# Hybrid trunk on one core: the folded attention matrices are built head by head inside the four mixer tiles

## The reference

```python
SEQ, D_MODEL, N_MEM, HEADS, D_FF = 2048, 1024, 256, 4, 2816
mem_n = rms_norm(mem, mem_norm)
h = rms_norm(x, mix_pre_norm)
zp, za, zg, zb, zc, zx = split(h @ w_in)          # 256, 384, 384, 384, 384, 384 columns
ya = pool_mixer(zp, pool_maps, pool_scale)        # causal means over 2, 4, 8, 16 rows
yb = silu(layer_norm(dwconv31(za * sigmoid(zg)) + b))
yc = zb * dwconv3(zc * zx)
x  = x + rms_norm(concat(ya, yb, yc) @ w_out, mix_post_norm)
h  = rms_norm(x, xattn_pre_norm)
q, k, v = h @ wq, mem_n @ wk, mem_n @ wv          # four heads of 256
x  = x + rms_norm(softmax(q k^T / 16) v @ wo, xattn_post_norm)
h  = rms_norm(x, ffn_pre_norm)
x  = x + rms_norm((silu(gate) * val) @ w_down, ffn_post_norm)   # gate, val = split(dwconv3(h @ w_up))
```

## Time and profile before

| what | value |
|---|---|
| median of three runs | 2834.37 us (2832.47 to 2837.37) |
| the profiled execution's own span | 2832.1 us, 2.3 us under that median |
| PE busy | 2597.2 us (92%), 11713 matmuls |
| DVE busy | 1672.2 us (59%) |
| ACT busy | 1035.4 us (37%) |
| POOL busy | 1226.4 us (43%), 462 lo subtractions of 2669 ns on average |
| mean DMA rate | 119 GB/s |

### The profile page before, as it was taken

One profiled execution on the slowest core, in us unless ns is written; L12 is line 12 of the kernel. 1 busy time (PEld: TensorE's weight loads), 2 busy tenths in 40 slices (PEclk: granted clock), 3 DMA queues, 4 the chain that ended last, 5 costly groups with the idle time before them and its releaser, 6 DMA issues.

```text
span 2832.1 us, 33905 instructions
## 1 busy us (share of the span) xinstructions
PE 2597.2 (92%) x11713; PEld 2143.7 (76%) x11713; DVE 1672.2 (59%) x2462; ACT 1035.4 (37%) x1624; POOL 1226.4 (43%) x469
## 2 busy tenths in 40 slices
PE   7978978969779989989999999899999999999997
PEld 7856766847657777777778887788877788878886
DVE  2498898998984364364642636706456246463362
ACT  4622323313234544444433343333433333333332
POOL 5565543634523334333443443344434534345342
PEclk9989989989989999999999999999999999999999
DMA  6634224342244244342532335233243323343231
GB/s 196 223 112 156 84 63 158 96 153 70 60 171 166 94 163 140 121 169 70 185 110 86 94 98 171 90 98 100 94 152 116 112 76 96 90 159 120 78 97 67
DMA packets 354500, 336.64 MB, mean 119 GB/s; under 512 B 12313, under 2 KB 278830, under 8 KB 354350
## 3 DMA queue, kind: packets, MB, share of 16 engines
q1 hardware_dynamic: 354349, 334.75, 37.0%
HBM read 300.10 MB, written 34.60 MB: 118 GB/s over the span
## 4 chain that ended last, share of the span: by engine, by line
PE 59%; issue 18%; DVE 18%; ACT 5%; DMA 0%; DVEq 0%; ACTq 0%
PE colb L1240 10%; PE colb L1242 10%; PE colb L1241 10%; PE accb L1240 9%; PE accb L1241 9%; PE accb L1242 9%; DVE arena L975 3%; PE colb L1274 2%; DVE xh L918 1%; ACT pair L531 1%; DVE small L844 1%; DVE small L842 1%; ACT junk L546 1%; DVE arena L1190 1%; DVE xh L850 1%
## 5 line engine op out<-in xcount | busy, mean ns | idle before, releaser
L502 POOL TENSOR_TENSOR pair<-raw,pair 128x1024 fp32r<-128x1024 f32 x462 | 1225.4, 2669 | 1569.7 <-ACT pair L531 1569.5
L1240 PE MATMUL colb<-hT,pair 128*128 128x512 f32 (+1 forms) x2080 | 814.2, 391 | 91.5 <-DVE arena L1039 46.1
L1241 PE MATMUL colb<-hT,pair 128*128 128x512 f32 (+1 forms) x2080 | 808.0, 388 | 0.0
L1242 PE MATMUL colb<-hT,pair 128*128 128x512 f32 (+1 forms) x2080 | 806.6, 388 | 0.0
L531 ACT ACTIVATE pair<-raw 128x1024 fp32r<-128x1024 f32 x462 | 481.4, 1052 | 411.5 <-PE accb L1242 290.3
L1240 PEld LDWEIGHTS colb<-hT,pair 128*128 128x128 f32 x2080 | 399.2, 192 | 185.9 <-issue 108.5
L1187 DVE TENSOR_SCALAR arena<-arena,par 128x512 f32<-128x512 f32 x176 | 239.0, 1398 | 447.6 <-ACT arena L774 442.2
L1240 PE MATMUL accb<-pair,act 128*128 128x512 f32 x1216 | 482.0, 396 | 3.9 <-DVE act L943 3.5
L1241 PE MATMUL accb<-pair,act 128*128 128x512 f32 x1216 | 477.2, 392 | 0.0
L1242 PE MATMUL accb<-pair,act 128*128 128x512 f32 x1216 | 476.7, 392 | 0.0
L1242 PEld LDWEIGHTS colb<-hT,pair 128*128 128x128 f32 x2080 | 398.7, 192 | 79.5
(11 more groups left out here) (119 smaller groups left out, 1946.7 us busy)
## 6 DMA issues: line engine op xcount, KB each, us to landing
raw<-in_ffn_w_up SPq DMA_DIRECT2D x176, 512.0 KB, 3.8
raw<-in_ffn_w_down SPq DMA_DIRECT2D x176, 256.0 KB, 2.9
raw<-in_w_in SPq DMA_DIRECT2D x68, 512.0 KB, 4.2
raw<-att_a SPq DMA_DIRECT2D x64, 256.0 KB, 3.1
raw<-att_b SPq DMA_DIRECT2D x64, 256.0 KB, 3.3
raw<-in_w_out SPq DMA_DIRECT2D x52, 256.0 KB, 2.9
xh<-in_x SPq DMA_DIRECT2D x4, 2048.0 KB, 10.5
xt<-in_x SPq DMA_DIRECT2D x4, 2048.0 KB, 15.5
```

Source lines behind the costliest of these rows:

```text
L502: nc.gpsimd.tensor_tensor(pair[:, b, 1, :], raw[:, r, :], pair[:, b, 0, :].bitcast(F32), ALU.subtract).then_inc(lo_done, 1)
L1240: nc.tensor.matmul(dst, sh, mh, start=first, stop=False)
L1241: nc.tensor.matmul(dst, sh, ml, start=False, stop=False)
L1242: return nc.tensor.matmul(dst, sl, mh, start=False, stop=last)
```

## The change

PREP keeps keys (8 slots), the conformer of the first tile (6), values (8) and the pool folding (2): 24 slots, where there were 40. Keys and values are stored to a DRAM tensor `kvd`, one 256 KB piece for each head and kind. Mixer tile t builds the parts of A and B that belong to head t: two slots q (the head's 256 columns of wq, four row blocks each), two slots o (the head's 256 rows of wo, half the columns each). A mixer tile has 29 slots in the place of 25, MIX_LAST 23 in the place of 19, and the new order of the first 21 is q0, r0, r1, q1, r2, r3, r4, r5, o0, o1, r6 to r10, out(0,0), out(0,1) (then c0 ...). All slots of the kernel together stay 462.

In a tile ACT copies both parts of the transposed wq, copies the four A and four B results to two `stage` buffers that now have space of their own (the arena held four before), and issues by itself eight stores and the loads of the next head's keys and values into `act`. RAWS goes from 4 to 3. The first rows of x are loaded ahead of the slots' stream; the memory rows go to `xt`, their transposes to `act`. DVE's corrections of the values (`key_values(1, ...)`) stand between the taps of the second conformer group of PREP.

The parts of the diff below are, in order: constants and orders of slots, the load of a head, PREP on SP (two parts), the mixer on ACT, PREP on DVE, the mixer on PE.

```diff
-RAWS = 4
+RAWS = 3
+STAGE_BUFS = 2
...
-    PREP_STEPS = [("b", 0), ("b", 1), ("rows", 0), ("b", 2), ("rows", 1), ("b", 3), ("conformer", 0),
-                  ("b", 4), ("b", 5), ("b", 6), ("b", 7), ("pooled", 0), ("pooled", 1)]
...
+    PREP_ORDER = [("k", i) for i in range(KD)] + [("c", i) for i in range(CSLOTS)] +\
+                 [("v", i) for i in range(KD)] + [("pooled", half) for half in range(2)]
+    MIX_HEAD = [("q", 0), ("r", 0), ("r", 1), ("q", 1), ("r", 2), ("r", 3), ("r", 4), ("r", 5), ("o", 0), ("o", 1)] +\
+               [("r", i) for i in range(6, RSLOTS)] + [("out", 0, 0), ("out", 0, 1)]
...
+        def load_head(eng, head, which):
+            eng.dma_start(act[:, :, HEAD_KV, :].bitcast(F32), kvd[bass.ds(head, 1), which].rearrange("o p s c -> (o p) s c"))\
+                .then_inc((k_in, v_in)[which], 16)
...
+            sp.dma_start(xh[:, :, :], rows(x_rows, 0)).then_inc(xh_in, 16)
...
+                        if k == 1:
+                            sp.wait_ge(kv_stored, 16 * 2 * HEADS)
+                            load_head(sp, 0, 0)
...
+                def a_rows(g):
+                    sc.wait_ge(xp_full, xp_at(p, t, ("A", g)) + 1)
+                    stage_out(p, t, ("A", g), g)
+                    staged(("A", g))
+                    sc.dma_start(att_a.rearrange("(k p) n -> p k n", p=P)[:, 2 * g:2 * g + 2, bass.ds(tile_of(p, t) * M, M)],
+                                 stage[:, g % STAGE_BUFS, :].rearrange("p (k n) -> p k n", k=2))\
+                        .then_inc(stage_stored[g % STAGE_BUFS], 16)
+                    if g == 3:
+                        load_head(sc, tile_of(p, t), 1)
+                def b_rows(half):
+                    n = place[p]["o", half]
+                    hi(p, t, n + AHEAD)
+                    for c in range(2):
+                        if c == 0:
+                            sc.wait_ge(xp_full, xp_at(p, t, ("B", half, 0)) + 1)
+                        else:
+                            slot_full(sc, p, t, n)
+                        stage_out(p, t, ("B", half, c), 4 + 2 * half + c)
+                        staged(("B", half, c))
+                        sc.dma_start(att_b[bass.ds(tile_of(p, t) * M + c * P, P), half * HALF:(half + 1) * HALF],
+                                     stage[:, c % STAGE_BUFS, :]).then_inc(stage_stored[c % STAGE_BUFS], 16)
+                    if half == 1 and p == MIX:
+                        load_head(sc, t + 1, 0)
+                wq_transposed(0)
+                rest(0)
+                a_rows(0)
+                a_rows(1)
+                rest(1)
+                wq_transposed(1)
+                rest(2)
+                a_rows(2)
+                a_rows(3)
+                for i in range(3, 6):
+                    rest(i)
+                b_rows(0)
+                b_rows(1)
+                rest(6)
+                round_y(5)
...
+                        if p == PREP and j == 1 and k % 3 == 2 and k // 3 < KD:
+                            key_values(1, k // 3, 3 * KD + 1 + k // 3)
...
+                wq_transposes(0)
+                rest(0)
+                a_rows(0)
+                a_rows(1)
+                rest(1)
+                wq_transposes(1)
+                rest(2)
+                a_rows(2)
+                a_rows(3)
+                for i in range(3, 6):
+                    rest(i)
+                pe.wait_ge(sums_ready, sums.at(p, t, 0))
...
+                b_rows(0)
+                b_rows(1)
+                for i in range(6, RSLOTS):
+                    rest(i)
```

More of the change, by code:

```diff
@@ new lines, in build @@
+    ITEMS = {PREP: PREP_ITEMS, MIX: MIX_ITEMS + [("c", i) for i in range(CSLOTS)], MIX_LAST: MIX_ITEMS}
+    item = {p: {what: i for i, what in enumerate(ITEMS[p])} for p in ITEMS}
+    MIX_XP = [w for w in MIX_ITEMS if w[0] in ("T", "A", "B", "row", "crow") and w not in (("T", 1, 1), ("T", 3, 1), ("B", 0, 1), ("B", 1, 1))]
+    PREP_XP = [w for w in PREP_ITEMS if w[0] in ("par", "mem", "bd", "row", "pooled") and w[2:] != (1,)]
+    xps = {PREP: PREP_XP, MIX: MIX_XP, MIX_LAST: MIX_XP}
+    SLOTS = [len(ORDER[PREP]), len(ORDER[MIX]), len(ORDER[MIX_LAST]), 2 * KD, 2 * KF + KF]
@@ L205, in uses_of, with xp_at @@
         return t * (COLS[p] // BANKS if TILES[p] > 1 else 0) + (col.base[p] + i) // BANKS
[L208 to L214, removed]
+    def xp_at(p, t, what):
+        return xp.at(p, t, xps[p].index(what))
+    STAGES = 8
+    PREP_STAGED = NP_ * 2
     PAR_ROWS = [("mem_norm", mem_norm, KD), ("mix_pre", mix_pre_norm, KD), ("att_pre", xattn_pre_norm, KD),
@@ L414, in _ @@
                 sp.dma_start(bd[o:o + PG, g * PG // P, o:o + PG], pool_maps[0, g]).then_inc(maps_in, 16)
[L415 to L425, removed]
@@ L695, in mix @@
+                rest(9)
+                round_y(1)
+                next_squares(p, t)
+                rest(10)
+                row0, xrow0 = item[p]["row", 0], xps[p].index(("row", 0))
+                hi(p, t, place[p]["out", 0, 0] + AHEAD)
                 round_y(6)
-                next_heads(p, t, 0, RSLOTS, range(4))
-                hi(p, t, RSLOTS + 1 + AHEAD)
+                next_heads(p, t, xrow0, row0, range(4))
+                hi(p, t, place[p]["out", 0, 1] + AHEAD)
                 round_y(7)
-                next_heads(p, t, 0, RSLOTS, range(4, KD))
+                next_heads(p, t, xrow0, row0, range(4, KD))
@@ new lines, in _, with conformer @@
+            banks_ready(PREP, 0, item[PREP]["mem", 0], KD)
+            for i in range(KD):
+                column_slot(PREP, 0, place[PREP]["k", i], item[PREP]["k", i], memT, M)
+            pe.wait_ge(maps_in, 16 * NW)
+            transposes(PREP, 0, item[PREP]["bd",], [bd[:, e, :] for e in range(NP_)]).then_inc(xp_full, 1)
+            pe.wait_ge(h_ready, 2)
+            for k in range(KD):
+                head(PREP, 0, item[PREP]["row", k], k)
+            def conformer(p, t):
+                banks_ready(p, t, item[p]["row", KD - BANKS], BANKS)
+                for i in range(CSLOTS):
+                    column_slot(p, t, place[p]["c", i], item[p]["c", i])
@@ new lines, in _ @@
+            conformer(PREP, 0)
+            for i in range(KD):
+                column_slot(PREP, 0, place[PREP]["v", i], item[PREP]["v", i], memT, M)
+            for half in range(2):
+                b = split_ready(PREP, 0, place[PREP]["pooled", half])
+                for g in range(NP_):
+                    dst = bank_free(PREP, 0, item[PREP]["pooled", half, g])
+                    ins = products(dst[:, :], [act[:, e, GF - 1, g * P:(g + 1) * P] for e in range(2)],
+                                   pieces(b, g * T, (g + 1) * T), True, True)
+                    ins.then_inc(slot_used if g else xp_full, 1)
```

496 lines of the change are left out of this document (222 added, 274 removed).

## The result

The changed kernel takes 2850.11 us (median of four runs, 2847.3 to 2851.03) where the kernel before, on the same chip, takes 2834.93: a ratio of 1.0055, with a 95% interval of 1.0043 to 1.0067. The forecast was 2853, slower. The profiled execution has a span of 2847.4 us, 15.3 more than 2832.1.

The account below looks back on a forecast made before the run. Mixer tiles were taken as bound by DVE. 2832.1 - 44.5 (prologue) + 3 (tile 0) + 55.8 (three tile starts) + 4 (raw buffers) = 2850.4 profiled; the runs' median lies 2.3 above: 2853 us, own range 2825 to 2888.

Parts of the forecast that it names:

- The prologue: Up to tile 0's statistics: DVE starts the first conformer at 73, not 137.34; statistics at 196, not 240.46: -44.5 us.
- hits: POOL subtractions of a weight split that meet DVE's work, each taken to cost 2.1 us.
- Tile 0: First mixer tile: no `x_new` to wait for, only the longer ACT chain: +3 us (0 to 16).
- The three tile starts: Starts of tiles 1, 2 and the last: each tile grows by 18.6 us, together +55.8 (41 to 90).
- The stall: At a tile's start DVE waits for `round_y(5)`, held on ACT by late r6 and r7: 16.0 us (13.7 to 22).
- The +0.5 for r10: Mixer tile: r10 may start that much behind its bank, since r9 ends near S + 46, S being when the sums are ready.
- Three raw buffers: ATTN and FFN: a load can start one slot, 5.5 us, later than with four buffers: +4 us (0 to 22).
- The cover is real but thin: Mixer tile: PE's added 9.2 us fit where it stood 13.0 idle before the sums; once gone, each microsecond costs one.
- rival C: As forecast, and PE also misses the sums: 8 us a tile for three tiles, 12 for the prologue: 2889; chance 0.12.
- A: Tile starts: ACT reaches `round_y(5)` by S + 24.4 (S: sums ready), so DVE does not stand; 2802 us, chance 0.22.
- B: DVE's wait at tile starts at its low end and the early start at its best: 2833 us, no change; chance 0.14.

Follow-up runs that it names:

- e5: The kernel before with POOL's subtraction over 512 of each weight slot's 1024 columns, half of the lo parts left at zero: 2626.97 us, ratio 0.9268.
- e7: The changed kernel with the values of the eight memory slots multiplied ahead of the first conformer, none between its taps: 2855.38 us, ratio 1.0075.
- e1: The changed kernel with SP running 13 slots ahead in the mixer tiles instead of 10: 2815.51 us, ratio 0.9937 to the kernel before.
- e2: The changed kernel with round_y(5) ahead of b_rows(0) in ACT's order, loads as they are: 2826.95 us, ratio 0.9973 to the kernel before.
- e4: The kernel before with three raw buffers in place of four, nothing else: 2832.43 us, ratio 0.9992.
- e12: The changed kernel with SP 13 slots ahead in the mixer tiles and POOL's subtraction at half width: 2661.05 us, ratio 0.9394 to the kernel before.

## Why the prediction was right

**The prologue, -44.5 forecast, -46.6 measured.** The first conformer starts at 76.62, not 73. The forecast gave it 19 hits, 40 us. In the changed kernel the excess over free durations is 26.2 us in its taps (84.5 less 87 x 0.67) and some 15 in the additions, copies and the short convolution behind it, 41 together. DVE's sums are ready at 179.7 (forecast 181), and PE comes to the transposes at 193.38 (forecast 194), so it is PE's chain that ends last, as was told: DVE waits 1.51 us for it at 193.90. e5 and e7 stand behind the price: a hit costs what the subtraction lasts, and an earlier start is mostly given back.

**Tile 0, +3 forecast, +7.6 measured.** Mis-sized, and within its bounds. The wait at L1005 is 5.14 us; tile 0 also has the four more subtractions, which I counted in the other tiles only.

**The three tile starts, +55.8 forecast, +60.2 measured** (21.8, 20.1 and 18.3). The stall: 16.0 forecast, 18.5 to 18.9 measured, by the steps that were told: r6 and r7 behind store, gain and `xh` (e1 takes that away and 16 of the 18.5 us go), and `round_y(5)` behind them (e2). Counted from the sums (361.1), r7 is split 36.8 us later and not 29.8, and DVE comes to L1005 30.8 us later and not 24.4; both moved by the 6.3 us by which `new_rows` lasts longer (below), so the difference between them held. From the split of r7 to the end of `round_y(5)` ACT took 12.5 us, where I had 10.6, above all since the wait for the first stage store was 3.12 and not 1.3. The hits: I took one more a tile. The records of the changed kernel show 3.4 us more of DVE's busy time, 1.6 hits; with the stall gone (e1) it is 7.9 us, nearly four. That fits what I had argued: subtractions that run while DVE stands cost nothing. The +0.5 for r10 is too small to be told apart.

**Three raw buffers, +4 forecast, no cost measured.** e4: ACT's waits for w_down more than double and the time does not move. ATTN is +1.0. FFN is -6.9 in the changed kernel and -7 in all its variants of full width, of which e4 accounts for 2.4 at most. PE's busy time is 6.0 us less (1433.9 against 1439.9), and the granted clock explains most of it: the changed kernel's FFN has three stretches at 1.2 GHz, 17 us, where before and e4 have six, 27 us, and by the same estimate as above they cost 5.5 us and not 10. Eleven records fewer are some 2 us. Why three of the stretches are gone stays open.

**The sum.** 46.6 gained and 67.8 lost in the mixer, 5.9 gained behind it; the forecast had 44.5 gained, 58.8 lost and 4 lost. The total hit 2853 within 3 us, and that closeness is luck: an error of 9 us in the mixer against 10 in ATTN and FFN and 2 in the prologue. What is not luck is the stall, its place and its size. The forecast's own range, 2825 to 2888, is not what its bounds add up to (2819 to 2934).

**A sign that was wrong.** I expected PE's transposes behind the conformer to wait for DVE 4 to 6 us. They don't wait at all, and PE comes late to them: the sums are ready at 361.1, 569.4 and 764.4, and the transposes start at 377.68, 571.1 and 780.7. So the step "The cover is real but thin" failed; PE had none. By the forecast's own sign this was rival C, but C's price of 8 us a tile did not come. POOL's and DVE's timelines at the first of the three:

```profile
339.64 26.14 POOL L528 TENSOR_TENSOR pair<-raw,pair 128x1024 fp32r<-128x1024 f32 x4 [3.77 <-ACT pair L557]
```

```profile
358.77 2.35 DVE L1043 COPY arena<-arena 128x30 f32<-128x30 f32 x1
361.04 0.15 DVE L975 TENSOR_TENSOR small<-small 128x4 f32<-128x4 f32 x1
361.22 2.24 DVE L906 TENSOR_SCALAR small<-small 128x4 f32<-128x4 f32 x1
363.50 2.31 DVE L907 TENSOR_SCALAR small<-small 128x4 int32<-128x4 int32 x1
365.85 0.17 DVE L908 TENSOR_SCALAR small<-small 128x4 int32<-128x4 int32 x1
366.05 2.32 DVE L910 TENSOR_TENSOR small<-small 128x4 f32<-128x4 f32 x1
```

The last group of taps (336.81 to 356.11) holds the first of POOL's four subtractions to its end, the others queue up, and PE stands 5.03 us, up to 358.40, for its lo part, and then works 6.8 us at a granted clock of 1.2 GHz: some 8 of its 16.6 us of lateness; the rest I have not taken apart. When the taps end, the subtractions run against the small operations of `new_rows`, which take 2.2 to 2.3 us in the place of 0.17. `new_rows` lasts 18.4 us in the place of 12.1, and PE's lateness lies beneath it and `sconv_chunk(0)`: DVE does not wait at the statistics (384.30). This is rival C's mechanism, present in this kernel and without a wait of DVE behind it, and in e12, with DVE's time cut, it takes 15.5 us at a time.

**The rivals.** A (no stall, 2802) is what e1 tried, and it gives 2815.5: the stall goes, but A had left 2.6 us a tile for the rest, and that rest is 9.6 on average in tiles 0 to 2, most likely since the subtractions that the stall had covered meet DVE again. B (the stall at its low end) did not happen: the stall was over its forecast. The rule of the Trainium skill (DMA: Bandwidth & Descriptors, Queues, rings and completion order), by which SP's and ACT's rings take turns, fits the trace: the first stage store, issued at 399.56, 6.6 us after `xt`'s 2 MB on SP's ring, had been waited for by 405.54. That is more than the 3.4 us of a store in the earlier trace rows and less than the forecast's 9.4 behind `xt`, and the stall is 18.5 and not 22. No run holds the store back on SP's ring, so this is no proof.

## What to carry to other kernels

When slots move back in a stream of loads, count which of them fall behind the large transfers at a tile's start, and look at what stands behind their first use on the engine that takes them: here four slots of shift put r6 behind a store of 2 MB and r7 and r8 behind 2.5 MB more, and three more slots of lead turned a loss of 0.55% into a gain of 0.6%. Starting a bound engine earlier gains less than the distance it moves if the work that contends with it then falls under it (28 us of start were 8.5 us of end). And measure a helper engine's operation by making it half as long: POOL is busy 43% of the time here and stands in no list of PE's waits of before by name, yet half its width is 7% of the kernel.

## What the runs showed of the hardware that I had not expected

POOL can wait for DVE over a whole run of short instructions. A subtraction that starts among the taps was at times held until the last tap had ended: in e12 some 17 us of 20.49 for one that takes 1.28 alone, in the changed kernel some 19 of the 26.14 at 339.64 (the rest is three more at 2.36), while the 29 taps ran in 19.30 us, 0.67 each, as if alone. In other groups the same subtraction got in, and cost DVE its own length. The Trainium skill (SBUF — State Buffer, Who interferes with whom) says that a DVE instruction with two SBUF inputs contends with a GpSimd instruction that reads SBUF, and that one in a 2-port perf mode contends too, that the port pair they share is an exclusive lock, and that the order of issue decides who blocks. The block of DVE for 2.1 us fits it, and so does L910, a 128x4 operation with two inputs that took 2.32 us; L906 and L907 have one input and took as long, and no row shows in which mode they ran. That section tells no case in which POOL gets no turn between 29 instructions, and I can't say from these runs what decides which of the two happens. The second surprise is how much of ATTN and FFN, 9% and 3.4%, hangs on the length of POOL's subtraction, with DVE busy less than half of the time there, and that part of it is the granted clock: once PE's gaps are gone the clock stands at 2.4 GHz all through e5's FFN (mean 1.00).
